# Fewer of the prompt's expert rows beside the sample's projections and self-attention

## The chip, the cores and the metric

The kernel runs on one core of a Trainium2 chip. The metric is the device time of one execution in microseconds (us); smaller is better. Engines are named as the profile names them: PE (TensorE matmuls), DVE (VectorE), ACT (ScalarE), POOL (GpSimd) and SP (SyncE, which only issues transfers here).

## What is computed

One encoder layer is applied to a prompt of 256 tokens and to a sample of 512 tokens, both 1024 wide, in float32. Each goes through a mixer (self-attention and a gated spatial branch), a cross-attention to 256 memory rows, and a feed-forward layer that picks experts; a last norm follows. The mixer and the feed-forward layer, cut to what the change touches:

```
proj = rmsnorm(x) @ w_in                 # 11 chunks of 512 columns: k v, q, u, v_sg, two gates
x += mix(self_attention(q, k, v), spatial_gating(u, v_sg), gates) @ w_out
x += cross_attention(...)
h = rmsnorm(x)
idx, g = top 16 of 16384 experts per token and head, 8 heads      # 128 experts per token
x += sum_k g_k * gelu(e_down[idx_k] . h) * e_up[idx_k]
```

## The kernel before

**Stages.** The prompt's pass comes first and stops after its experts are chosen. Then the sample's pass runs through six stages, `mixer_inputs`, `self_attention`, `mixer_outputs`, `cross_inputs`, `cross_attention` and `routing_and_gates`. A last stage, `experts`, computes the outputs of both. Every engine has its own program; semaphores order them.

**The prompt's rows.** Each of the prompt's two tiles of 128 tokens has 128 experts, so 256 steps are to be done, and a step is called a row here: POOL gathers one row of `e_down` for each of 128 tokens (128 x 1024 floats, 512 KB, line 167), and DVE multiplies it with `H` and adds it up into one column of `dots` (line 153, followed by a short read of its accumulator). Rows sit in a ring of nine buffers (`row_ring`; five of them until row 32), so POOL can be at most nine rows ahead of DVE. All of this is done beside the sample's pass: `bg.dve(dve, n)` at a place in DVE's program means "do the next n rows here", and the counts are written out by hand at each place. Rows are taken in order, up to 256 in all, so a row that is left out at one place is done at a later one. `bg.finish` (line 2101) does all that are left; it stands in `routing_and_gates` after the first three calls of `pick_experts`, which take up to six rows each.

**The sample's projections** (`mixer_inputs`). The weights of a chunk come in two halves. For each half, SP loads 1 MB (`w_raw`), ACT rounds it (`w_hi`, line 231), DVE makes the rest (`w_lo`, line 239) and PE runs three products of it with four token tiles (lines 262 to 264). From chunk 3 on ACT moves each tile's result to one of three buffers (`stage`, line 756) or to `Y`, and SP stores it to DRAM (a spill). The fourth tile of a chunk therefore waits until the spill of the first has landed. DVE's program for chunk c is: rows, `w_lo` of a half, rows, `w_lo` of the next (function `aside`).

**The sample's self-attention.** Its 32 steps, each with two heads and one token tile, run as a pipeline. In step s, PE does the scores of s (line 1065), turns the probabilities of s-2 (line 1078) and multiplies those of s-3 with the values (line 1090). DVE takes the row maximum of s (line 1158), scales the probabilities of s-1 (lines 1143, 1146), and then may do a row. ACT copies the turned probabilities of s-3 (line 1124) and does the exponentials of s (line 1115). Once in four steps ACT and DVE also take out a finished block of outputs (lines 1132 and 1153).

**The routing** (`routing_and_gates`). PE projects the queries of the expert choice in four chunks and scores them (line 1761); ACT copies the scores out (line 1837), the last eight of sixteen into ring buffers that must have given up their rows first. DVE picks experts in 18 calls of `pick_experts`. Before call 6 it writes `T_sum` (line 2104, shown as `ahead`), the sum of two halves of the activations, which needs the last projection to be over. After its last scores PE waits for `T_sum` and then computes eight blocks ahead (line 1798), turns the first tile's choices, and ACT and DVE build gate matrices from them (lines 1869, 2088, 2093).

Of the kernel before, what the change touches and what calls it, by code (L numbers as in the profile page):

```python
# [620 lines left out]
def mixer_inputs(nc, block, st, q, bg, x_in, T, Y, qT, kT, v_sb, lin, tr, A, U, GA, GS, stage, ident, gains, choice=None, norm=None, routed=None):  # L621
# [4 lines left out]
    with ExitStack() as ctx:  # L626
# [12 lines left out]
        SOFTEN = 7  # L639
# [14 lines left out]
        ROWS_AT = {x: bg.NARROW for x in ((3, 1), (4, 1), (5, 0), (6, 0), (6, 1))} | {(10, 1): 3}  # L654
# [109 lines left out]
        def _(dve):  # L764
# [65 lines left out]
            def aside(c, half):  # L830
                if not q.first:
                    if (c, half) == (3, 0):
                        choice.list(dve, 0)
                    if (c, half) == (6, 1):
                        choice.list(dve, 1)
                    bg.dve(dve, ROWS_AT.get((c, half), 5 if c >= SOFTEN else 0))
                    r = {(1, 0): 3, (2, 0): 4, (3, 0): 5, (4, 0): 6, (4, 1): 7, (5, 1): 8}.get((c, half))
                    if r is not None:
                        choice.rank(dve, r)
                    if r == choice.units:  # L840
                        choice.shift(dve)
                    if (c, half) == (SOFTEN + 1, 0):
                        choice.finish(dve)

            for c in range(11):
                aside(c, 0)
                st.split_lo(dve, H + 2 * c + 2)
                aside(c, 1)
                for t in range(NT):
                    n = c * NT + t  # L850
                    if n < NQ:
                        nh = 4 if c == 0 else 8
                        dve.wait_ge(sq_done, n + 1)
                        if n == 0:
                            dve.memset(hss[:], 1.0).then_inc(hs_done, 1)
                            dve.wait_ge(hs_done, 1)
                        dve.tensor_reduce(hss[:, n % 2, 0:nh],
                                          sq[:, n % 2, 0:nh * HD].rearrange("p (h f) -> p h f", h=nh),
                                          AX_X, ALU.add).then_inc(hs_done, 1)
                        dve.wait_ge(hs_done, n + 2)  # L860
                        dve.tensor_scalar(hms[:, n % 2, :], hss[:, n % 2, :], 1.0 / HD, EPS, ALU.mult,
                                          ALU.add).then_inc(ms_done, 1)
                        if t >= 1:
                            rotate(n - 1)
                        if t == NT - 1:
                            st.split_lo(dve, H + 2 * c + 3)
                            rotate(n)
                if c >= 3:
                    st.split_lo(dve, H + 2 * c + 3)
# [169 lines left out]
def self_attention(nc, block, q, bg, T, qT, kT, v_sb, ident, lin, tr, projected):  # L1039

    with ExitStack() as ctx:
# [96 lines left out]
        @block.vector  # L1138
        def _(dve):
            def norm(p):  # L1140
                i = p % 3
                dve.wait_ge(exped, 2 * p + 2)
                dve.reciprocal(rr[:, i, :], rs[:, i, :]).then_inc(inverted, 1)
                dve.wait_ge(inverted, p + 1)
                for e in range(2):
                    dve.tensor_scalar(probs[:, i, e, 0:w], probs[:, i, e, 0:w], rr[:, i, e:e + 1], None,
                                      ALU.mult).then_inc(normed, 1)

            for step in range(N + 4):
                for n in range(NH // 2):  # L1150
                    if step == block_end[n] + 3:
                        dve.wait_ge(out_hi, n + 1)
                        dve.tensor_tensor(T[1][:, n, 0:w], tr[:, n % 2, 0:w], T[0][:, n, 0:w].bitcast(F32),
                                          ALU.subtract).then_inc(out_lo, 1)
                if step < N:
                    i = step % 3
                    dve.wait_ge(scored, 2 * step + 2)
                    dve.tensor_reduce(nmx[:, i, :], lin[:, 2 * (step % 2):2 * (step % 2) + 2, 0:w], AX_X, ALU.max,
                                      negate=True).then_inc(negated, 1)
                if 1 <= step < N + 1:  # L1160
                    norm(step - 1)
                if step % 4 != 0:
                    bg.dve(dve, 1)

        @block.gpsimd
# [1485 lines left out]
```

## Time and profile before

| | us |
|---|---|
| median of three runs | 2590.58 |
| the three runs | 2585.24, 2590.58, 2592.02 |
| the profiled execution | 2600.45 |
| its span, first to last instruction | 2598.7 |
| busy in it: PE, DVE | 2455.0 (94%), 2179.8 (84%) |
| busy in it: POOL, ACT | 1387.4 (53%), 1095.8 (42%) |
| the 256 row steps on DVE, line 153 | 312.5 |

The profiled execution took 9.9 us more than the median. The stages of the sample's pass follow each other, so each is read by itself: what PE does in it, what it waits for, and which engine's work ended last before PE went on. A row of a timeline has the start, the duration, the engine, the line and the operation, what is written from what, and in brackets how long the engine sat idle before it and what ended that wait.

### The profile page before, as it was taken

To read this page: it belongs to the slowest core of one execution; us is meant where nothing else is said; L and a number is where in the kernel's file an instruction comes from. 1 tells how busy PE (TensorE), PEld (TensorE's weight loads), DVE (VectorE), ACT (ScalarE), POOL (GpSimd) and SP (SyncE) were. 2 spreads that over 40 slices of the span, in tenths; PEclk is the share of its full clock that TensorE was granted. 3 is DMA by queue.
4 is the path that set the end of the run, shared out by engine and by line. 5 is a ranking of instruction groups with operands and counts; after the bars stand their busy time and mean duration, and the time that the engine had idled before them with its cause. 6 is when DMAs were issued, how large, how long until landed. Compare 5 with 4: busy or idle time off the path is not lost.

```text
span 2598.7 us, 38804 instructions
## 1 busy us (share of the span) xinstructions
PE 2455.0 (94%) x13113; PEld 2071.4 (80%) x13113; DVE 2179.8 (84%) x3950; ACT 1095.8 (42%) x1938; POOL 1387.4 (53%) x1054
## 2 busy tenths in 40 slices
PE   7989999989999999999998889999999999999998
PEld 6767889878776778777866668888888888888887
DVE  7356546998679898877878979999999999999999
ACT  5464544332257323342328983333333333343333
POOL 0000000347641554645655538888887877778785
PEclk9999999999999999999999999999999999999999
DMA  7736536467973897977834559999999999999998
GB/s 266 272 116 219 194 131 226 168 238 291 354 275 115 308 334 275 346 258 258 327 115 152 214 219 402 401 406 407 412 415 415 415 414 415 415 414 393 411 404 314
DMA packets 240422, 787.50 MB, mean 303 GB/s; under 512 B 21904, under 2 KB 75328, under 8 KB 219552
## 3 DMA queue, kind: packets, MB, share of 16 engines
q0 software_dynamic: 112288, 408.77, 40.5%
q1 hardware_dynamic: 128000, 377.00, 39.0%
q8 instruction: 77, 1.26, 0.2%
q14 instruction: 57, 0.47, 0.0%
HBM read 728.01 MB, written 57.67 MB: 302 GB/s over the span
## 4 chain that ended last, share of the span: by engine, by line
PE 34%; DVE 21%; issue 18%; DMA 12%; ACT 10%; POOL 4%; POOLq 0%; DVEq 0%; SPq 0%; ACTq 0%
PE lin L262 8%; PE lin L264 8%; PE lin L263 8%; ACT row_ring L1869 4%; DVE w_lo L239 3%; DMA G<-in_downT 3%; DMA rows<-in_up,now 3%; DMA w_raw<-in_wall 3%; DVE Y L2497 2%; DVE row_ring L153 2%; ACT w_hi L231 2%; DVE H L2497 2%; PE tr L1798 2%; DVE low L2463 1%; POOL rows L2356 1%
## 5 line engine op out<-in xcount | busy, mean ns | idle before, releaser
L167 POOL DMA_INDIRECT row_ring<-in_down,IDX x256 | 356.1, 1391 | 312.7 <-DVE dots L153 244.2
L239 DVE TENSOR_TENSOR w_lo<-w_raw,w_hi 128x2048 fp32r<-128x2048 f32 x100 | 231.8, 2318 | 227.9 <-ACT w_hi L231 222.2
L262 PE MATMUL lin<-w_hi,T_hi 128*128 128x512 f32 x976 | 389.4, 399 | 25.4 <-DVE w_lo L239 8.2
L264 PE MATMUL lin<-w_hi,T_lo 128*128 128x512 f32 x976 | 387.8, 397 | 0.0
L263 PE MATMUL lin<-w_lo,T_hi 128*128 128x512 f32 x976 | 385.4, 395 | 0.0
L231 ACT ACTIVATE w_hi<-w_raw 128x2048 fp32r<-128x2048 f32 x116 | 222.0, 1914 | 364.7 <-PE lin L264 323.2
L2356 POOL DMA_INDIRECT rows<-in_up,now x192 | 308.0, 1604 | 64.1 <-issue 55.8
L153 DVE CUSTOM_DVE_ANT_0 row_ring<-row_ring,H 128x1024 f32<-128x1024 f32 x256 | 312.5, 1262 | 24.1 <-DMA row_ring<-in_down,IDX 23.7
L2356 POOL DMA_INDIRECT w_raw<-in_up,now x189 | 285.0, 1508 | 82.6 <-issue 45.5
L262 PE MATMUL lin<-w_hi,c_hi 128*128 128x512 f32 x768 | 309.1, 403 | 20.4 <-DVE c_lo L2510 20.2
L263 PE MATMUL lin<-low,c_hi 128*128 128x512 f32 x768 | 307.0, 400 | 0.0
L262 PE MATMUL tr<-T_hi,w_hi 128*128 128x384 f32 x896 | 303.6, 339 | 2.2 <-DVE low L2463 2.2
L264 PE MATMUL lin<-w_hi,c_lo 128*128 128x512 f32 x768 | 304.7, 397 | 0.0
L263 PE MATMUL tr<-T_lo,w_hi 128*128 128x384 f32 x896 | 300.8, 336 | 0.0
L264 PE MATMUL tr<-T_hi,low 128*128 128x384 f32 x896 | 300.0, 335 | 0.0
L262 PEld LDWEIGHTS lin<-w_hi,T_hi 128*128 128x128 f32 x976 | 184.4, 189 | 76.4 <-DVE w_lo L239 13.6
L263 PEld LDWEIGHTS lin<-w_lo,T_hi 128*128 128x128 f32 x976 | 184.5, 189 | 43.4
L264 PEld LDWEIGHTS lin<-w_hi,T_lo 128*128 128x128 f32 x976 | 184.0, 189 | 42.4
L2433 ACT ACTIVATE c_hi<-gl 128x384 fp32r<-128x384 f32 x128 | 67.1, 524 | 344.3 <-DVE gl L2507 344.2
L2497 DVE SCALAR_TENSOR_TENSOR Y<-rows,dots,Y 128x1024 f32<-128x1024 f32 x160 | 202.1, 1278 | 3.6 <-DMA rows<-in_up,now 3.3
L2497 DVE SCALAR_TENSOR_TENSOR Y<-w_raw,dots,Y 128x1024 f32<-128x1024 f32 x157 | 198.0, 1276 | 6.6 <-DMA w_raw<-in_up,now 6.6
L262 PEld LDWEIGHTS lin<-w_hi,c_hi 128*128 128x128 f32 x768 | 146.3, 191 | 57.1 <-DVE c_lo L2510 27.3
(318 smaller groups left out, 5270.3 us busy)
## 6 DMA issues: line engine op xcount, KB each, us to landing
w_raw<-in_wall SPq DMA_DIRECT2D x116, 1024.0 KB, 6.9
row_ring<-in_up SPq DMA_DIRECT2D x128, 512.0 KB, 10.4
G<-in_downT SPq DMA_DIRECT2D x112, 512.0 KB, 10.9
wd<-dense_gates SPq DMA_DIRECT2D x32, 768.0 KB, 21.2
weight_rests<-w_lo SPq DMA_DIRECT2D x16, 1024.0 KB, 4.9
w_lo<-weight_rests SPq DMA_DIRECT2D x16, 1024.0 KB, 6.2
dense_gates<-peer SPq DMA_DIRECT2D x6, 2048.0 KB, 6.7
dense_gates<-w_raw SPq DMA_DIRECT2D x5, 2048.0 KB, 6.9
```

Source lines behind the costliest of these rows:

```text
L153: dve.tensor_tensor_reduce(self.ring[:, k, :], self.ring[:, k, :], self.H[:, r // NE, :], 1.0, 0.0, ALU.mult, ALU.add, self.dots[:, col:co ...
L167: pool.indirect_dma_start(self.ring[:, k, :], None, self.table, bass.IndirectOffsetOnAxis(ap=self.IDX[:, col:col + 1], axis=0)).then_inc(s ...
L231: act.activation(self.hi[:, h % 2], self.raw[:, h % 2], ACT.Copy).then_inc(self.hi_done, 1)
L239: dve.tensor_tensor(self.lo[:, h % 2], self.raw[:, h % 2], self.hi[:, h % 2].bitcast(F32), ALU.subtract).then_inc(self.lo_done, 1)
L262: pe.matmul(out, lhs[0], rhs[0], start=start, stop=False, skip_group_check=True)
L263: pe.matmul(out, lhs[0], rhs[1], start=False, stop=False, skip_group_check=True)
L264: return pe.matmul(out, lhs[1], rhs[0], start=False, stop=stop, skip_group_check=True)
L1798: last = pe.matmul(tr[:, n % 2, 0:DENSE], ahead_raw[:, n % 2, k, :], T_sum[:, k, :], start=(k == 0), stop=(k == KB - 1), skip_group_check= ...
L1869: last = act.activation(hot1[:, r % 2, k, :], mark1[:, r % 2, k // 2, :, k % 2], ACT.Copy, scale=pairs[:, i, 2, col:col + 1])
L2356: pool.indirect_dma_start(rows[k], None, table, bass.IndirectOffsetOnAxis(ap=now[:, j % 2, k:k + 1], axis=0)).then_inc(rows_in[k], 16)
L2433: act.activation(c_hi[:, b % 2, :], gl[:, b % 2, :], ACT.Copy).then_inc(c_hid, 1)
L2497: dve.scalar_tensor_tensor(out=into, in0=source, scalar=dots[:, bass.ds(first_row + r, 1)], in1=into, op0=ALU.mult, op1=ALU.add).then_inc( ...
```

## The change

Two counts are lowered. From chunk 7 of the sample's projections on, four rows are done per half chunk where there were five (the last half chunk keeps its three). In the sample's self-attention a row is done in the even steps, where it was done in every step but each fourth.

```diff
-                    bg.dve(dve, ROWS_AT.get((c, half), 5 if c >= SOFTEN else 0))
+                    bg.dve(dve, ROWS_AT.get((c, half), 4 if c >= SOFTEN else 0))
...
-                if step % 4 != 0:
+                if step % 2 == 0:
                     bg.dve(dve, 1)
```

In the projections seven half chunks lose a row each. In the 36 rounds of the attention loop 27 rows become 18. So 16 rows are done later: every later count stays as it is, the ends of the three calls of `pick_experts` take one more, and `bg.finish`, which had nothing left to do, gets 15.

DVE in the self-attention, before, steps 6 and 7 of the loop, counted from 0 (`att_nmx` is the row maximum, `att_probs` the scaled probabilities, `T_lo` the block taken out):

```order
L1158 TENSOR_REDUCE att_nmx<-lin 128x2
L1143 RECIPROCAL att_rr<-att_rs 128x2
L1146 TENSOR_SCALAR att_probs<-att_probs,att_rr 128x512 x2
L153 ISA row_ring,dots<-row_ring,H 128x1024
L153 ISA dots 128x1
L1153 TENSOR_TENSOR T_lo<-tr,T_hi 128x512
L1158 TENSOR_REDUCE att_nmx<-lin 128x2
L1143 RECIPROCAL att_rr<-att_rs 128x2
L1146 TENSOR_SCALAR att_probs<-att_probs,att_rr 128x512 x2
L153 ISA row_ring,dots<-row_ring,H 128x1024
```

The same place after the change, up to the start of step 8:

```order
L1158 TENSOR_REDUCE att_nmx<-lin 128x2
L1143 RECIPROCAL att_rr<-att_rs 128x2
L1146 TENSOR_SCALAR att_probs<-att_probs,att_rr 128x512 x2
L153 ISA row_ring,dots<-row_ring,H 128x1024
L153 ISA dots 128x1
L1153 TENSOR_TENSOR T_lo<-tr,T_hi 128x512
L1158 TENSOR_REDUCE att_nmx<-lin 128x2
L1143 RECIPROCAL att_rr<-att_rs 128x2
L1146 TENSOR_SCALAR att_probs<-att_probs,att_rr 128x512 x2
L1158 TENSOR_REDUCE att_nmx<-lin 128x2
```

Of four steps, the one ahead of `T_lo` keeps its row (step 6 here), the one of `T_lo` and the second after it lose theirs (7 and 9), and the step between those gets one that it did not have (8).

POOL in the routing, before, from the second call of `pick_experts` on (`cand` and `id_b` are POOL's part of a call; `x4` is four gathers in a row):

```order
L167 DMA row_ring<-in_down,IDX 128x1024 x4
L2186 TENSOR_TENSOR cand<-best 128x2x64
L2186 TENSOR_TENSOR cand<-best 128x2x48
L2190 CAST id_b<-ids 128x64
L2164 TENSOR_TENSOR pick<-pick,id_b 128x4x16x16
```

After the change, the end of the third call and what follows it:

```order
L167 DMA row_ring<-in_down,IDX 128x1024
L2186 TENSOR_TENSOR cand<-best 128x2x64
L2186 TENSOR_TENSOR cand<-best 128x2x48
L2190 CAST id_b<-ids 128x64
L167 DMA row_ring<-in_down,IDX 128x1024 x9
L2164 TENSOR_TENSOR pick<-pick,id_b 128x4x16x16
```

Before, POOL's last gathers were the four ahead of the second `cand`. Now five stand there and fifteen follow, the last nine of them between `id_b` of the third call and the look-up behind it. On DVE the 16 rows more stand together, behind the third call of `pick_experts` and ahead of the fourth.

## Rows read from the trace of the kernel before

**Rows 1.** Chain that ended last, 1150 to 1600: start, us, engine and line

```profile
1331.04 41.56 PE tr L1798 x128
```

**Rows 2.** DVE in order of time, routing stage

```profile
1234.01 1.22 DVE L153 CUSTOM_DVE_ANT_0 row_ring<-row_ring,H 128x1024 f32<-128x1024 f32 x1
1235.15 1.22 DVE L153 CUSTOM_DVE_ANT_0 row_ring<-row_ring,H 128x1024 f32<-128x1024 f32 x1
...
1294.78 1.36 DVE L153 CUSTOM_DVE_ANT_0 row_ring<-row_ring,H 128x1024 f32<-128x1024 f32 x1
...
1307.82 0.30 DVE L2027 MAX8 best<-row_ring 128x8 f32<-128x128 f32 x1 [3.65 <-ACT row_ring L1837]
...
1325.74 3.43 DVE L2104 TENSOR_TENSOR ahead<-T_hi,T_lo 128x1536 f32<-128x1536 f32 x2 [1.71 <-PE lin L264]
```

**Rows 3.** PE in order of time, same stage

```profile
1331.04 6.39 PE L1798 MATMUL tr<-ahead,H 128*128 128x384 f32 x19 [0.69 <-ACT row_ring L1837]
```

**Rows 4.** POOL in order of time there, and a gather's time to landing (1280 to 1345)

```profile
1239.79 1.99 POOL L167 DMA_INDIRECT row_ring<-in_down,IDX  x1 [0.30 <-issue]
...
1246.88 0.95 POOL L167 DMA_INDIRECT row_ring<-in_down,IDX  x1 [0.30 <-issue]
...
1295.01 1.23 POOL L2190 CAST id_b<-ids 128x64 bf16<-128x64 uint32 x1
...
row_ring<-in_up,IDX POOLq DMA_INDIRECT x3, 4.5
```

**Rows 5.** Projections: busy time by engine; what PE waited for, 660 to 742

```profile
660.00:706.00 46.00, 41.73 (x177) 32.55 (x176) 29.52 (x42) 11.09 (x11) 28.26 (x21) 1.00 0.98 365
...
PE lin L262 <- DVE w_lo L239: 2.2, 2, 1.1
PE lin L262 <- ACT stage L756: 2.1, 2, 1.1
```

**Rows 6.** Projections, chunk 7, in order of time: DVE, SP's queue, ACT

```profile
658.57 1.23 DVE L153 CUSTOM_DVE_ANT_0 row_ring<-row_ring,H 128x1024 f32<-128x1024 f32 x1 [3.56 <-DMA row_ring<-in_down,IDX]
659.72 2.29 DVE L239 TENSOR_TENSOR w_lo<-w_raw,w_hi 128x2048 fp32r<-128x2048 f32 x1
...
662.41 12.25 SPq L670 DMA_DIRECT2D attn_gate_rows<-stage  x4
...
673.72 0.60 ACT L756 ACTIVATE stage<-lin 128x512 f32<-128x512 f32 x1 [10.86 <-DMA attn_gate_rows<-stage]
```

**Rows 7.** Self-attention, one period of four steps: length; busy PE, PEld, DVE, ACT, POOL

```profile
799.00:812.75 13.75, 12.82 (x132) 9.52 (x130) 12.47 (x23) 10.19 (x26) 2.84 (x3) 1.00 0.38 114
```

**Rows 8.** Self-attention, the same period in order of time: PE and DVE

```profile
798.34 1.13 PE L1065 MATMUL lin<-kT,G 64*128 64x256 f32 x8
799.54 1.23 DVE L1158 TENSOR_REDUCE att_nmx<-lin 128x2 f32<-128x1024 f32 x1 [1.13 <-PE lin L1065]
...
801.60 1.14 PE L1065 MATMUL lin<-kT,G 64*128 64x256 f32 x8
802.82 1.22 DVE L1158 TENSOR_REDUCE att_nmx<-lin 128x2 f32<-128x1024 f32 x1
...
806.64 1.12 PE L1078 MATMUL lin<-ident,att_probs 128*128 128x128 f32 x8 [0.55 <-ACT att_probsT L1124]
...
808.71 1.13 PE L1065 MATMUL lin<-kT,G 64*128 64x256 f32 x8
```

**Rows 9.** Self-attention, its start, in order of time: DVE, then PE

```profile
744.63 0.17 DVE L1143 RECIPROCAL att_rr<-att_rs 128x2 f32<-128x2 f32 x1 [0.39 <-ACT att_probs L1115]
...
746.77 1.22 DVE L1158 TENSOR_REDUCE att_nmx<-lin 128x2 f32<-128x1024 f32 x1
...
750.11 1.93 PE L1078 MATMUL lin<-ident,att_probs 128*128 128x128 f32 x8 [2.23 <-ACT att_probsT L1124]
751.97 1.84 PE L1090 MATMUL tr<-att_probsT,v_sb 128*64 128x128 f32 x16
...
755.83 1.09 PE L1090 MATMUL tr<-att_probsT,v_sb 128*64 128x128 f32 x16
```

## The prediction

> **What bounds the kernel now.** I read the busy times first, then the chain that ended last, then each stage that the change touches: what PE waits for in it, and which engine DVE, ACT and POOL wait for. The reader is to see that a row on DVE costs the kernel something only where PE is waiting for what stands behind it. There are three such places to look at, and they differ.
>
> In the projections PE is busy 41.73 of 46 us around chunks 7 and 8 [rows 5]. It stops four times between 660 and 742, 4.3 us together: twice for `w_lo`, twice for a bank that ACT has not emptied. Both follow from one event. The fourth tile of chunk 7 waits 10.86 us on ACT for a spill to land [rows 6]; behind it stand `w_hi` and `w_lo`. That spill was issued at 662.41, because SP first waits for a `w_lo` that began at 659.72, and DVE began that late because its fifth row waited 3.56 us for its gather. The DMA engines are busy 98% of that stretch [rows 5].
>
> In the self-attention four steps take 13.75 us, with PE busy 12.82 and DVE 12.47 of them [rows 7]. Both look full, so the order in time decides. The scores begin at 801.60 and the row maximum at 802.82, right behind a row. Where DVE was idle the same pair is 798.34 and 799.54 [rows 8]. So the row made the maximum 0.02 us late (1.22 against 1.20). From there the chain goes over the exponentials, the copies of the finished block and of the turned probabilities, PE's turn at 806.64, which waited 0.55 us for it, and the scores at 808.71. A loop through ACT and PE sets the pace, two steps long; the rows fit in almost exactly.
>
> In the routing PE has 41.56 us on the chain that ended last, the blocks ahead [rows 1]. They began at 1331.04, released by ACT's last score copy after 0.69 us [rows 3]. They also need `T_sum`, which DVE began at 1325.74 and ended 3.43 us later [rows 2], at 1329.2, 1.9 us before. DVE had no row left by then: the last began at 1294.78 [rows 2].
>
> **The change part by part.** I sum against the profiled execution, 2600.45 us, and carry the sum over to the median of the runs shown, 2590.58.
>
> *Routing, 16 rows more.* Two rows follow each other at 1234.01 and 1235.15 [rows 2]: 1.14 us each, 18.3 us for 16. All stand ahead of `T_sum`. DVE was idle between its last row and `T_sum` for 3.65 us (waiting for a score copy) and 1.71 us (for the last projection) [rows 2]; a later DVE finds both ready, so 5.4 us are covered. `T_sum` ends 12.9 us later, at 1342.1. PE, which was released 1.9 us behind it, begins 11.0 us later. DVE's longer waits behind `T_sum` cover nothing: what they wait for comes after PE's blocks and moves with them.
>
> To this come the gathers. Nine are now queued on POOL behind `id_b`, which ended at 1296.2 (1295.01 and 1.23) [rows 4], while DVE does the 16 rows from 1296.1 (1294.78 and 1.36, less the overlap) to 1314.4. While DVE runs rows back to back a gather takes 1.99 us and 0.30 to the next, otherwise 0.95 and 0.30; where the DMA engines have little to do it lands 4.5 us after its start [rows 4]. If all are there in time this costs nothing. If POOL needs four slow pitches of 2.29 and, with DVE waiting now and then, four of about 1.7, the ninth gather starts at 1312.2, lands at 1316.7, and its row ends at 1317.9, 3.5 us late. A stretch of 16 rows is nearest to the slow pitch; I take 2.6, bounds 0 and 3.5. ACT's copy of the ninth score tile waits for row 251 too. It may hold PE's last projection by a microsecond or two, but PE waits for `T_sum` behind that, so I cost it at nothing.
>
> Last, PE stands idle for some 13 us and then starts slowly. After 2.23 us of idling in the attention a turn took 1.93 us and the values 1.84 [rows 9], where they take 1.12 [rows 8] and 1.09 [rows 9]: 1.6 us, with bounds 0 and 1.6. Together 11.0 + 2.6 + 1.6 = 15.2, bounds 11.0 and 16.1.
>
> *Projections, seven rows fewer.* The row that waited 3.56 us for its gather was the fifth of its half chunk, so `w_lo` need no longer wait for it, and SP's spill can go up to 3.6 us earlier. One gather in five is gone from DMA engines that were 98% busy. PE's two stops in a chunk are worth 2.1 us together, and the spill has to land that much earlier for both to vanish. I take 4.0 of the 4.3 us [rows 5]; bounds 0 and 4.3. Behind that stands PE itself, which runs without a gap.
>
> *Self-attention, nine rows fewer.* In the loop the row behind `T_lo` is not on the two-step chain, and those that are cost it 0.02 to 0.05 us in a period: 0.4 us in seven periods. At the start the maximum of step 2 begins at 746.77, behind the row of step 1. Now a row stands ahead of the maximum of step 1 instead, and the gain is the 0.39 us that DVE idles at 744.63 today [rows 9]. So 0.8 us, bounds 0 and 2.4: the upper end holds if PE's idle time shrinks enough that the 1.6 us of slow start go as well.
>
> Sum: 15.2 - 4.0 - 0.8 = +10.4 us; bounds 11.0 - 4.3 - 2.4 = +4.3 and +16.1. The profiled execution would take 2610.9, the median 2601.0.
>
> **Rivals.**
>
> *DVE paces the self-attention.* Then a row fewer in each of eight periods gives back up to 1.14 us, capped by PE's 0.93 us of idle time in a period (13.75 less 12.82 [rows 7]): 7.4 us in place of 0.4. The sum is +3.4 us, 2594.0: not slower by a measurable amount. It decides from 0.4 us a period on. For it: DVE is busy 91%. Against it: the 0.02 us above, and that PE's wait names ACT. The Trainium skill, "Perfetto Trace Analysis" (Identifying the Most-Contended Engine), would have it: it compares DVE's occupancy with PE's weight loads rather than its matmuls, here 12.47 against 9.52 us [rows 7], and says to optimize the engine with the most.
>
> *The moved rows are covered.* If PE's blocks did not need `T_sum`, or DVE's idle time before it were 18 us and not 5.4, only the gains would be left: 2590.6 - 4.8 = 2585.8. The wait is in the code, and DVE's idle times are read, so little speaks for it.
>
> *The gathers starve.* POOL might not get on at all while DVE runs. DVE then does the seven rows that are already in the ring (to 1304.1), and only then nine gathers start, 1.25 us apart: the ninth at 1314.1, landed at 1318.6, its row done at 1319.7, 5.3 us late. The sum is 11.0 + 5.3 + 1.6 - 4.8 = +13.1, 2603.7; with no gain in the projections, as spills also queue with weight loads, +17.1 and 2607.7. For it: gathers do slow down beside DVE's rows. Against it: they went on at 1.99 us [rows 4]. The Trainium skill, "SBUF — State Buffer" (SBUF: two separate sides), would have it: the port pair that DVE and GpSimd share is an exclusive lock and the loser blocks fully. The trace differs so far, slowed and not stopped.
>
> **How the numbers follow.** My forecast has a chance of 0.66 (2594.9 to 2606.7 by its bounds), DVE as the pacer 0.14, covered rows 0.07, starved gathers 0.13. The measurement can tell 0.3% from no change, about 7.8 us: up to 2598.4 counts as the same. My forecast lies above that in about eight cases of ten (0.52) and within it otherwise; starved gathers always above. DVE as the pacer is the same. Covered rows are mostly the same, since 4.8 us is less than 7.8; I leave 0.04 for faster, for a larger gain upstream than I see. That gives faster 0.04, same 0.31, slower 0.65. The range runs from 2592, which takes in the pacer, to 2607.5.
>
> **What would show it.** In the changed profile `T_sum` (line 2104) ends 13 to 16 us later against the end of the projections, DVE has no idle time ahead of it, and PE's first block ahead waits for DVE for about 13 us where ACT released it. The waits for `stage` and `w_lo` between 660 and 742 are gone or halved. The self-attention's period stays between 13.6 and 13.75 us. It would be wrong if PE's blocks began with no wait for DVE, or if the period fell to 13.3 or less.

## The result, and the profile after

The changed kernel takes 1.0047 times as long as the one before (95% interval 1.0030 to 1.0063): a median of 2604.65 us over 12 runs against 2591.6 us. By the ratio that is 12.2 us more, 7.8 to 16.3 by the interval (the two medians differ by 13.05), where the prediction had 10.4 more. Single executions of one kernel spread by 6 to 10 us to either side, so what follows counts a stage in the traces and the whole in ratios. The two profiled executions differ by 12.6 us in span (2611.3 against 2598.7).

The chain that ended last shows in the routing what was forecast; its columns are the start, the length and the engine and line:

```profile
1330.44 9.80 issue
1340.24 44.27 PE tr L1798 x128
```

The same blocks took 41.56 us before [rows 1], and the 9.80 us ahead of them are new. "issue" means that the profile names no releaser for that wait. DVE in order of time names it (start, duration, what, and in brackets the idle time ahead and what ended it):

```profile
1296.33 1.21 DVE L153 CUSTOM_DVE_ANT_0 row_ring<-row_ring,H 128x1024 f32<-128x1024 f32 x1
...
1302.66 1.23 DVE L153 CUSTOM_DVE_ANT_0 row_ring<-row_ring,H 128x1024 f32<-128x1024 f32 x1 [5.11 <-DMA row_ring<-in_down,IDX]
...
1311.20 1.22 DVE L153 CUSTOM_DVE_ANT_0 row_ring<-row_ring,H 128x1024 f32<-128x1024 f32 x1
...
1336.58 3.55 DVE L2104 TENSOR_TENSOR ahead<-T_hi,T_lo 128x1536 f32<-128x1536 f32 x2
```

`T_sum` ends at 1340.13 and PE goes on at 1340.24. DVE's two idle spells ahead of it [rows 2] are gone, as forecast, but there is a new one of 5.11 us, for a gather.

PE's restart is the third part. PE in order of time has it waiting 10.44 us:

```profile
1340.24 6.20 PE L1798 MATMUL tr<-ahead,H 128*128 128x384 f32 x10 [10.44 <-issue]
```

It had already stood 5.32 us in the last projection, for ACT's copy of the ninth score tile:

```profile
1306.99 1.41 PE L1761 MATMUL tr<-peer 128*128 128x128 f32 x5 [5.32 <-ACT row_ring L1837]
```

The windows view behind the wait of 10.44 us gives the length, the busy time of PE, PEld, DVE, ACT and POOL, the granted clock, the DMA share and GB/s:

```profile
1340.20:1343.20 3.00, 2.96 (x5) 1.78 (x6) 3.00 (x20) 0.00 (x0) 1.15 (x3) 0.50 0.28 67
1343.20:1346.20 3.00, 3.00 (x6) 1.60 (x6) 3.00 (x23) 0.00 (x0) 2.92 (x2) 0.57 0.27 111
1346.20:1354.00 7.80, 7.80 (x25) 4.56 (x24) 7.80 (x55) 0.92 (x2) 6.02 (x10) 1.00 0.49 160
```

PE ran for most of 6 us at the lower level, 1.2 GHz (0.50), and the 128 products took 2.7 us more.

Upstream, the same view for chunks 7 and 8, and then for a period of the attention:

```profile
656.00:702.00 46.00, 45.96 (x198) 36.55 (x197) 29.52 (x42) 14.97 (x15) 28.40 (x21) 1.00 1.00 386
...
786.90:800.60 13.70, 12.81 (x128) 9.49 (x129) 11.49 (x22) 10.16 (x26) 2.06 (x3) 1.00 0.26 78
```

PE is now busy all of the first stretch, where it had been busy 41.73 of 46 us [rows 5]. In the second DVE lost one row's time (11.49 us in place of 12.47 [rows 7]) and the period stayed.

The account of the two executions, each mark a start on PE (the first score of the routing, line 1761, at 1250.6 and 1242.3; the first turned choice, line 1781, at 1372.4 and 1384.3):

| stretch | before | after | difference |
|---|---|---|---|
| to 544.79 / 548.31, nothing changed there | 544.8 | 548.3 | +3.5 |
| to 584.27 / 583.83, a weight load from DRAM | 39.5 | 35.5 | -4.0 |
| to the attention's first scores | 153.7 | 150.3 | -3.5 |
| the attention, to its last scores | 108.2 | 106.0 | -2.2 |
| to the cross-attention's first scores | 283.2 | 280.9 | -2.3 |
| to the routing's first scores | 121.2 | 121.3 | +0.1 |
| routing, to the first turned choice | 121.8 | 142.0 | +20.2 |
| the rest | 1226.3 | 1227.0 | +0.7 |

The first two rows belong to the executions and not to the change: chunk 7 comes later, and the second stretch took 35.6 us with the attention's half alone, where nothing is changed up to there, and 38.7 in a kernel with the whole change (`weights_after_gather`, below). So does the -2.3: with one row of the attention moved and every later row in its place (`start_row_moved`) the stretch took 280.6 us.

### The profile page after: what moved, and what is told of

The parts are those of the page before. It is cut to its first block, busy times and chain, and to the rows that moved or that the text cites. A ratio compares the mean times of both kernels' runs of the same rounds, so it can differ in the third digit from the quotient of the medians.

```text
span 2611.3 us, 38804 instructions
## 1 busy us (share of the span) xinstructions
PE 2457.7 (94%) x13113; PEld 2070.8 (79%) x13113; DVE 2181.4 (84%) x3950; ACT 1095.6 (42%) x1938; POOL 1381.3 (53%) x1054
## 4 chain that ended last, share of the span: by engine, by line
PE 27%; DVE 27%; issue 19%; DMA 12%; ACT 10%; POOL 5%; DVEq 0%; SPq 0%; POOLq 0%; ACTq 0%
PE lin L262 6%; PE lin L264 6%; PE lin L263 6%; ACT row_ring L1869 4%; DVE Y L2497 3%; DVE w_lo L239 3%; DMA G<-in_downT 3%; DMA w_raw<-in_wall 3%; DVE row_ring L153 2%; DMA rows<-in_up,now 2%; DVE rows L2483 2%; DVE w_raw L2483 2%; DVE low L2463 2%; DVE low L2474 2%; PE tr L1798 2%
## 5 line engine op out<-in xcount | busy, mean ns | idle before, releaser
L2356 POOL DMA_INDIRECT rows<-in_up,now x192 | 296.2, 1543 | 70.6 <-issue 56.2
```

The lines of the kernel that those rows point to most:

```text
L2356: pool.indirect_dma_start(rows[k], None, table, bass.IndirectOffsetOnAxis(ap=now[:, j % 2, k:k + 1], axis=0)).then_inc(rows_in[k], 16)
```

## The experiments

**One half each.**

```diff
projections_only:
-                    bg.dve(dve, ROWS_AT.get((c, half), 5 if c >= SOFTEN else 0))
+                    bg.dve(dve, ROWS_AT.get((c, half), 4 if c >= SOFTEN else 0))
attention_only:
-                if step % 4 != 0:
+                if step % 2 == 0:
```

> Only the projections give up a row per half chunk; the attention keeps three rows in four steps, so 7 rows move to the routing. Theory A (rows ahead of T_sum cost what DVE's two idle spells of 5.4 us and T_sum's slack of 1.9 us don't cover): 7 x 1.14 = 8.0 us, of which 7.3 are covered, so +0.7; the projections give back 3.5 to 4.0; the sum is -3, about 2589 us, up to 2594 if the last gathers are late by 5 us as in the changed kernel. Rival B (nothing is covered, each row costs its 1.14 us and the gathers are late in every case): +8.0 + 5.1 - 3.5 = +9.6, about 2601.

Measured: 0.9996 (0.9982 to 1.0011), -1.0 us.

> Only the attention gives up rows; the projections keep five, so 9 rows move to the routing. Theory A: 9 x 1.14 = 10.3 us less 7.3 covered = +3.0, late gathers 0 to 5.1, PE's slow restart 0 to 2.7, less 2.2 in the attention: +0.8 to +8.6, 2592 to 2600, likeliest 2596. Rival B (nothing is covered): +10.3 + 5.1 + 2.7 - 2.2 = +15.9, about 2607. By A the two halves together cost less than the whole change, since each uses the same 7.3 us of cover; by B their effects add up to more than the whole.

Measured: 1.0041 (1.0026 to 1.0057), +10.6 us; at 2591.6 that is 2602, 2598.3 to 2606.4 by the interval. That is a little above theory A's range, which the interval overlaps; B's 2607 lies only just outside it. So the ratio hardly tells the two apart, and the traces have to. These are the lines of the first scores and of the blocks ahead (first and last start stand ahead of the semicolon). Before:

```profile
L1761 PE MATMUL tr<-peer x128: 270/275/377, 1250.6 to 1330.1; 128*128 128x128 f32 x128
L1798 PE MATMUL tr<-ahead,H x256: 486/486/590, 1331.0 to 1534.1; 128*128 128x384 f32 x128
```

After:

```profile
L1761 PE MATMUL tr<-peer x128: 270/275/553, 1242.3 to 1329.5; 128*128 128x128 f32 x128
L1798 PE MATMUL tr<-ahead,H x256: 486/486/978, 1340.2 to 1546.0; 128*128 128x384 f32 x128
```

The projections alone:

```profile
L1761 PE MATMUL tr<-peer x128: 270/275/377, 1237.2 to 1316.7; 128*128 128x128 f32 x128
L1798 PE MATMUL tr<-ahead,H x256: 486/486/847, 1319.1 to 1523.9; 128*128 128x384 f32 x128
```

The attention alone:

```profile
L1761 PE MATMUL tr<-peer x128: 269/275/376, 1246.3 to 1325.8; 128*128 128x128 f32 x128
L1798 PE MATMUL tr<-ahead,H x256: 485/487/977, 1333.9 to 1539.1; 128*128 128x384 f32 x128
```

From first score to first block it takes 80.4 us before; 81.9 (+1.5) with 7 rows more, 87.6 (+7.2) with 9, 97.9 (+17.5) with 16. Rows at 1.14 us less 7.3 us of cover make 0.7, 3.0 and 11.0. What is left, 0.8, 4.2 and 6.5, is nearly what DVE waited for gathers: nothing, then 3.67 us in the attention's kernel, then 5.11 and 0.5 between the rows. The 0.5 to 0.9 us left in each case aren't accounted for. So the cover is there once, and a stretch of rows behind the last `id_b` waits for its gathers. DVE with the attention's half alone:

```profile
1305.03 1.23 DVE L153 CUSTOM_DVE_ANT_0 row_ring<-row_ring,H 128x1024 f32<-128x1024 f32 x1 [3.67 <-DMA row_ring<-in_down,IDX]
```

**The gathers taken out.** In `Rows`, the last nine rows are neither gathered nor waited for:

```diff
-            dve.wait_ge(self.arrived[k], 16 * len(self.in_slot(k, r + 1)))
+            dve.wait_ge(self.arrived[k], 16 * len(self.in_slot(k, min(r + 1, self.end - 9))))
+            if r >= self.end - 9:
+                dve.wait_ge(self.used, r - 8)
...
+            if r >= self.end - 9:
+                self.asked = r + 1
+                continue
```

> The changed kernel, but the last nine rows work on what lies in the ring, so the nine gathers of 512 KB behind the third call are left out and DVE never waits for them; DVE's work is the same. Theory A with late gathers as a term: DVE's wait of 5.1 us ahead of those rows and about 0.7 us of waits between them vanish, T_sum is 6 us earlier and so is PE: about 2599. Rival D (the gathers' wait only fills time that T_sum or PE would wait anyhow): no change, about 2604.

Measured: 1.0025 (1.0010 to 1.0041), where the change had 1.0047: 5.7 us less, 6 expected. The two intervals overlap, so it is the trace that decides. Its lines stand five further down (2109 is `T_sum`, 1803 the blocks ahead). DVE, then PE:

```profile
1328.68 3.56 DVE L2109 TENSOR_TENSOR ahead<-T_hi,T_lo 128x1536 f32<-128x1536 f32 x2
```
```profile
1332.33 4.07 PE L1803 MATMUL tr<-ahead,H 128*128 128x384 f32 x7 [12.08 <-issue]
```

PE follows `T_sum` (1332.24) at once again, 92.2 us after its first score at 1240.1: +11.8 against before. That is the price of the 16 rows by themselves, and `T_sum` is the wait: moved 5.7 us, it moved PE by 5.7.

**Why that gather was late.** POOL in the changed kernel's trace, the first three and the last of the nine:

```profile
1290.89 1.76 POOL L167 DMA_INDIRECT row_ring<-in_down,IDX  x1 [0.15 <-issue]
1292.96 1.97 POOL L167 DMA_INDIRECT row_ring<-in_down,IDX  x1 [0.30 <-issue]
1295.23 1.99 POOL L167 DMA_INDIRECT row_ring<-in_down,IDX  x1 [0.30 <-issue]
...
1303.77 0.94 POOL L167 DMA_INDIRECT row_ring<-in_down,IDX  x1 [0.30 <-issue]
```

POOL went on: the last of the nine began 12.9 us after the first. DVE does the last nine rows from 1296.33 on, the first of them without a wait. The row at 1302.66 is the second of the nine, so its gather began at 1292.96 and was there 9.7 us later; the one ahead of it took 5.2. The DMA queues of the same kernel (packets, MB, share of the 16 engines) and the gather issued there (time to landing), from 1293 to 1295:

```profile
q0 software_dynamic: 103, 0.42, 74.8%
row_ring<-in_down,IDX POOLq DMA_INDIRECT x1, 9.7
```

And from 1295 to 1297:

```profile
q1 hardware_dynamic: 41, 0.34, 62.9%
q0 software_dynamic: 46, 0.12, 16.4%
```

In the first the gathers (q0) moved 0.42 MB alone. Then SP's last half of `w_lo` (q1, 1 MB, issued at 1294.0) was served too, and the gathers got 0.12. The Trainium skill, "DMA: Bandwidth & Descriptors" (Queues, rings and completion order), says that a DMA engine goes round the queues that have work, packet by packet; the trace agrees, with both queues moving in one stretch. To try it, SP loads that half only once the first of the nine has been used:

```diff
-            st.load(sp, H0 + 2, H0 + 2 * (W_END - W_XO) + 2)
+            st.load(sp, H0 + 2, H0 + 2 * (W_END - W_XO) + 1); sp.wait_ge(bg.used, bg.end - 8)
+            st.load(sp, H0 + 2 * (W_END - W_XO) + 1, H0 + 2 * (W_END - W_XO) + 2)
```

> The changed kernel, but SP loads the last half of w_lo (1 MB, issued at 1294.0 in the changed kernel's trace) only when the first of the last nine gathers has been used. Theory E (that gather landed 9.7 to 11.8 us after its issue because the weight load was served along with it): DVE's wait of 5.1 us ahead of those rows falls to 2 us or less, T_sum and PE are some 3 us earlier, ratio to the kernel before about 1.0035 where the changed kernel had 1.0047. Rival F (POOL's pace beside DVE sets it): DVE's wait stays at about 5 us, and the time too.

Measured: 1.0035 (1.0020 to 1.0049). DVE:

```profile
1300.44 1.28 DVE L153 CUSTOM_DVE_ANT_0 row_ring<-row_ring,H 128x1024 f32<-128x1024 f32 x1 [1.21 <-DMA row_ring<-in_down,IDX]
1306.47 1.23 DVE L153 CUSTOM_DVE_ANT_0 row_ring<-row_ring,H 128x1024 f32<-128x1024 f32 x1 [4.75 <-DMA row_ring<-in_down,IDX]
```

The wait for the second gather fell to 1.21 us, as theory E has it, with POOL at the same pace (1.97 and 1.99 us for the second and third gather, as in the changed kernel), so the weight load was its cause. But nothing is won: the load, issued at 1299.26, is now served along with the third gather, and that row waits 4.75 us. PE began its blocks 99.0 us after its first score (1244.0 to 1343.0), not earlier than the 97.9 of the change, and its first turned choice came 142.0 us after that score in both; the lower ratio lies within the other's interval.

**The rows put elsewhere.** The whole change, with its 16 rows done where DVE had waited for ACT:

```diff
-                    bg.dve(dve, 4 if (j, c) == (2, 1) else 8)
+                    bg.dve(dve, {(0, 0): 11, (1, 0): 9, (2, 0): 9, (2, 1): 7}.get((j, c), 8))
-                bg.dve(dve, 3 if h % 2 == 0 else 2)
+                bg.dve(dve, 3 if h % 2 == 0 or h == 5 else 2)
-                bg.dve(dve, 7 if h < 13 else 3)
+                bg.dve(dve, {10: 9, 13: 6}.get(h, 7))
-                bg.dve(dve, ROWS_XO)
+                bg.dve(dve, ROWS_XO + 2 * (c == 0))
```

> The whole change, but the 16 rows are done between the attention and the routing, at places where DVE waits for ACT's w_hi (3 + 1 + 1 + 3 in the mixer's outputs, 1 + 2 + 3 in the cross-attention's inputs, 2 at the routing's start), so that the last stretch ahead of T_sum is the one of the kernel before. Theory A (the loss is all in the routing): the routing's cost vanishes and the gains upstream stay, -3.5 in the projections and -2.2 in the attention: about 2586, 2584 to 2589. Rival C (those gaps aren't free, since DVE would be late for w_lo or the gathers, up to 16 x 1.14 us): 2592 to 2604.

Measured: 1.0013 (0.9996 to 1.0030). The routing's cost is gone (80.5 us from first score to first block), but theory A's 2586 was missed. DVE in order of time:

```profile
1118.99 1.23 DVE L153 CUSTOM_DVE_ANT_0 row_ring<-row_ring,H 128x1024 f32<-128x1024 f32 x1 [4.02 <-DMA row_ring<-in_down,IDX]
...
1179.19 1.23 DVE L153 CUSTOM_DVE_ANT_0 row_ring<-row_ring,H 128x1024 f32<-128x1024 f32 x1 [5.79 <-DMA row_ring<-in_down,IDX]
```

PE's two longest waits from the cross-attention to the first turned choice (total, times, longest):

```profile
PE lin L945 <- DVE xatt_probs L1009: 4.4, 1, 4.4
PE lin L356 <- DVE G L435: 4.1, 1, 4.1
```

They were 1.0 and 2.0 us in the kernel before. An idle gap on DVE is free only if the gather for it has landed. At these two places it had not (the second wait for a gather was 3.98 us long in the kernel before, with two rows fewer there), and from the cross-attention to the routing's first scores it took 129.1 us in place of 121.2. A further 2.1 us went in the blocks ahead, which now waited for `H` from DRAM.

**The two upstream gains by themselves.** First the projections' change with its 7 rows in the mixer's outputs:

```diff
-                    bg.dve(dve, ROWS_AT.get((c, half), 5 if c >= SOFTEN else 0))
+                    bg.dve(dve, ROWS_AT.get((c, half), 4 if c >= SOFTEN else 0))
-                    bg.dve(dve, 4 if (j, c) == (2, 1) else 8)
+                    bg.dve(dve, {(0, 0): 11, (1, 0): 9, (2, 1): 7}.get((j, c), 8))
```

> Only the projections give up their 7 rows; these are done in the mixer's outputs (3 + 1 + 3), where the kernel with all 16 rows in gaps lost nothing up to the cross-attention. Theory A: PE's stops of some 4.3 us in chunks 7 and 8 go and nothing is added: about 2584.5, ratio 0.9983. Rival (the projections' stops only move, or another wait takes their place): ratio 1.000.

Measured: 0.9982 (0.9969 to 0.9996). PE's waits from 600 to 742 hold no stop for `stage` behind a weight half any more and 0.2 us for `w_lo` (and 0.7 us for a weight load from DRAM):

```profile
PE lin L262 <- DVE w_lo L239: 0.2, 1, 0.2
```

With five rows a half chunk (the attention's half alone) they are still there:

```profile
PE lin L262 <- DVE w_lo L239: 3.0, 3, 1.1
PE lin L262 <- ACT stage L756: 1.7, 2, 1.3
```

Then the attention's order alone:

```diff
-                if step % 4 != 0:
+                if step % 4 != 0 and step != 1 or step == 0:
```

> The kernel before, with the attention's row of step 1 done in step 0; no row leaves the attention. Theory A (what the attention gains, it gains at its start, 0.4 us of DVE's idling and perhaps the 1.6 us in which PE restarts slowly): -0.4 to -2.0 us, and a period of 13.75 us as before. Rival (the gain is in the loop, by fewer rows in each period): no change.

Measured: 0.9992 (0.9976 to 1.0008), which tells nothing apart. The traces do. The turn that waited 2.23 us on PE in the kernel before [rows 9], in this kernel:

```profile
751.50 1.12 PE L1078 MATMUL lin<-ident,att_probs 128*128 128x128 f32 x8 [1.43 <-ACT att_probsT L1124]
```

And with the projections' half alone, which has the old order:

```profile
743.16 1.12 PE L1078 MATMUL lin<-ident,att_probs 128*128 128x128 f32 x8 [2.23 <-ACT att_probsT L1124]
```

The wait falls from 2.23 to 1.43 us with no row taken out of the attention. The turn itself took 1.12 us in both, where it had taken 1.93 in the kernel before: that part does not hang on the order alone.

Both together, and then both with the rows at other places, since PE had waited 1.98 us for DVE behind the three rows added at (0, 0):

> Both: the projections' 7 rows in the mixer's outputs and the attention's row of step 1 done in step 0. Theory A: -4.3 - 0.4 to -4.3 - 2.0, about 2583, ratio 0.998. Rival as for the two parts: 1.000.

Measured: 0.9971 (0.9955 to 0.9988), 7.5 us less than before.

```diff
-                    bg.dve(dve, 4 if (j, c) == (2, 1) else 8)
+                    bg.dve(dve, {(1, 0): 9, (2, 0): 9, (2, 1): 7}.get((j, c), 8))
-                bg.dve(dve, 3 if h % 2 == 0 else 2)
+                bg.dve(dve, 3 if h % 2 == 0 or h == 5 else 2)
-                bg.dve(dve, 7 if h < 13 else 3)
+                bg.dve(dve, {10: 8, 13: 3}.get(h, 7))
```

> As the kernel with both halves that was faster than the one before, but none of the 7 rows stands ahead of the first w_lo of the mixer's outputs, where DVE then waited 5.0 to 5.5 us for a gather and PE 2.0 us for DVE; they are done at 1 + 1 + 3 later places of the mixer's outputs and 1 + 1 of the cross-attention's inputs. Theory A (a row is free where neither DVE nor its gather makes PE wait): 2 us less than that kernel, ratio to the kernel before about 0.9963. Rival (the rows of these places are late there too): 0.997 or more.

Measured: 0.9983 (0.9968 to 0.9998). PE's wait there, with the projections' rows at (0, 0):

```profile
901.29 7.11 PE L1244 MATMUL lin<-Y,sgw 128*128 128x512 f32 x16 [1.98 <-DVE G L1302]
```

And without rows there:

```profile
899.59 7.11 PE L1244 MATMUL lin<-Y,sgw 128*128 128x512 f32 x16 [0.31 <-DVE G L1302]
```

The wait went, as theory A has it; the 2 us don't show in the ratio, whose interval takes in both kernels. Both are faster than the one before by their intervals, the second only just; which of them is better is open.

## Why the prediction was right, point by point

- **The path through `T_sum`** held. `T_sum` had no idle time ahead of it but for gathers, and PE began 0.1 us behind it. The 11.0 us for 16 rows (16 times 1.14 is 18.2 and not 18.3, which leaves the 11.0 as it is) measured 11.8 where no gather could be late.
- **The gathers** are the step that failed: 2.6 us with bounds 0 and 3.5, measured 5.7. It took POOL's slow pitch for the limit and a landing time of 4.5 us from a stretch in which the DMA engines had little to do. POOL had three slow pitches and then five of 1.25 us; the second gather landed late, not the ninth, because a weight load came between. The 5.3 us of the rival with starved gathers fit the size, but not by its mechanism: POOL issued at 1292.96 and 1295.23 while DVE did rows, slower but not stopped, where the page that spoke for that rival ("SBUF — State Buffer" of the Trainium skill, SBUF: two separate sides) has the loser block fully while the other's instruction runs.
- **ACT's ninth score copy** was named, and its size missed: it held PE for 5.32 us, not "a microsecond or two", and PE restarted slowly. It cost nothing all the same, since `T_sum` came later, as the prediction had it. But it put two of the signs out: PE's wait ahead of the blocks was 10.4 us and not about 13, and `T_sum` ended 11.5 us later against the end of the projections (ACT's copy behind the last one began at 1325.74 before and 1325.19 after), not 13 to 16.
- **The slow restart** was 1.6 us with 1.6 as its upper bound, read from a wait of 2.23 us. After 10.4 us it was 2.7. The length of the wait alone doesn't set it: the same blocks, 41.56 us before, took 1.7 us more behind a wait of 2.14 us in the kernel with the projections' half, and 1.6 more behind 9.89 us in `weights_after_gather`. These two:

```profile
1319.08 43.23 PE tr L1798 x128
```
```profile
1343.01 43.18 PE tr L1798 x128
```

- **The projections**: 4.0 of 4.3 us was forecast, and the account has 3.5. The four stops are gone, and with the rows in the mixer's outputs the gain is 0.9982, 4.7 us (1.0 to 8.0). The 3.5 us of the two executions are the low end: from the same weight load to the attention's first scores it took 153.7 to 156.7 us in the three kernels with five rows and 147.9 to 150.6 in the eight with four, 5.6 less in the mean and above the bound of 4.3. A second weight load, for which PE stood 0 to 3.0 us, differs among them; the rest is open.
- **The attention**: the loop was right, 13.72 us (PE's turns at 773.17 and 786.89) against 13.75, and so DVE was not the pacer, although it was busy 91%. The rule of the Trainium skill that was weighed there, "Perfetto Trace Analysis" (Identifying the Most-Contended Engine), to go for the engine with the highest occupancy, found no gain in this loop. The start gained 2.05 us (from the first scores to the turn behind which the waits repeat, 738.00 to 765.39 before and 734.10 to 759.44 after), near the upper bound of 2.4 and not the 0.8 taken: PE's wait fell to 1.43 us, and the slow start of 1.6 us was gone. Only the first part is shown to be the order's. With the old order and a quick turn (the projections' half alone, 731.06 to 756.89) it took 25.8 us, against 25.3 to 25.6 with the new one: about 0.4, as the prediction had it. The slow turn stood in two of the three traces with the old order and in none of the eight with the new.
- **The sum**: 11.8 + 5.7 + 2.7 = 20.2 in the routing in place of 15.2, above the routing's own upper bound of 16.1; 3.5 and 2.2 upstream in place of 4.8. The two misses, 5.0 and 0.9, have opposite signs. These terms make 14.5 us; the executions' own differences (-2.0 in the account above) and its rounding lead from there to the 12.6 of the spans, and the 12 runs gave 12.2, 1.8 above the forecast. That the total came so near is in part luck: the routing cost more than was thought possible, and the rest of the kernel gave more back.

The other rivals fell: the moved rows were not covered, and a row fewer in each period moved nothing.

## What to carry to other kernels

Before background work is moved to a later stage, read that stage for its cover: the idle time of the engine ahead of the wait that ends last, plus that wait's slack, is free once, and here 7.3 us of it took 6 of 16 rows. The work's own supply moves with it: a gap on the engine is free only if the transfer that the work needs has landed, and a row's transfer is priced by what else the DMA engines carry just there. A busy share of 91% does not make an engine the pacer; a loop that did not change when a row left it (13.75 and 13.72 us) says so.

## What had not been expected of the hardware

A gather of 512 KB took 9.7 us from its start to its use, where the one ahead of it took 5.2 and one lands after 4.5 us with little else on the DMA engines [rows 4], because 1 MB of weights was served along with it; put off, the load made DVE wait 4.75 us for the gather after it instead. And the same wait of PE does not always end in the same clock: after 2.23 us ahead of the attention's turn, the 3 us around it ran at a granted clock of 0.69 in the kernel before and of 1.00 with the projections' change alone, and the turn took 1.93 and 1.12 us. With that half and its rows in the mixer's outputs the clock was 0.71 again, and the turn took 1.72. Why is open. The windows of before (749 to 752) and of the projections' half alone (742 to 745):

```profile
749.00:752.00 3.00, 1.89 (x10) 1.59 (x10) 2.96 (x7) 1.96 (x5) 0.94 (x1) 0.69 0.97 397
```
```profile
742.00:745.00 3.00, 1.83 (x22) 1.62 (x24) 2.96 (x7) 2.16 (x6) 0.94 (x1) 1.00 0.67 236
```
